# Expert rows gathered in quarters with dealt channels, and turned by VectorE instead of TensorE

## What is computed

```python
h = rmsnorm(x, g_norm_ffn) * (1.0 + sc2) + sh2          # one row of 1024 channels a token
lg = x @ w_router_grp + b;  gsel = argmax(lg)            # 1 of 4 groups
le = x @ w_router_exp + b   # the 8 experts of the group, softmax, top 2, weights renormalised
for e in range(32):                                      # SwiGLU, EXPERT_FF = 256
    hid = silu(x @ w_exp_gate[e]) * (x @ w_exp_up[e])
    out = out + combine[:, e:e + 1] * (hid @ w_exp_down[e])
x = x + gt2 * out;  y = rmsnorm(x, g_final)
```

## Time and profile before

| | |
|---|---|
| median of 3 runs | 1409.73 us (1407.08, 1409.73, 1416.6) |
| the profiled execution | 1413.11 us |
| its span in the trace | 1411.4 us |
| mean granted TensorE clock | 0.973 of 2.4 GHz |
| TensorE busy | 1327.9 us (94%), weight loads 795.0 us |
| VectorE, ScalarE, POOL busy | 606.3 us, 323.3 us, 117.9 us |
| moved | 243.47 MB in 121473 packets, mean 173 GB/s |
| out projection to slot table | 890 to 1052 us of the span |
| the 23 rounds | first product at 1060.95, last at 1333.58 |
| loop block and final norm | to the end |

### The profile page before, as it was taken

One profiled execution on the slowest core, in us unless ns is written; L12 is line 12 of the kernel. 1 busy time (PEld: TensorE's weight loads), 2 busy tenths in 40 slices (PEclk: granted clock), 3 DMA queues, 4 the chain that ended last, 5 costly groups with the idle time before them and its releaser, 6 DMA issues. The chain is left out here.

```text
span 1411.4 us, 21105 instructions
## 1 busy us (share of the span) xinstructions
PE 1327.9 (94%) x8689; PEld 795.0 (56%) x8689; DVE 606.3 (43%) x1290; ACT 323.3 (23%) x692; POOL 117.9 (8%) x135
## 2 busy tenths in 40 slices
PE   5899999999999999999999999999959999999976
PEld 3344448876667666666567666788853333333322
DVE  6743452324342144950482244434653632222247
ACT  4200002545443210122322222111211011111013
POOL 0000001030000051010000000000010000000042
PEclk9999999999999999999999999999968999999997
DMA  9425324321002362422413084610076999999878
GB/s 363 126 90 166 110 90 157 126 78 42 27 19 74 99 213 72 148 62 61 84 56 141 16 272 121 232 64 31 30 276 231 365 374 408 418 417 414 344 244 240
DMA packets 121473, 243.47 MB, mean 173 GB/s; under 512 B 23159, under 2 KB 87303, under 8 KB 112137
## 3 DMA queue, kind: packets, MB, share of 16 engines
q1 hardware_dynamic: 98368, 191.69, 38.1%
q10 hardware_dynamic: 14690, 28.26, 5.4%
q0 software_dynamic: 8320, 22.17, 5.2%
HBM read 208.30 MB, written 37.07 MB: 174 GB/s over the span
## 5 line engine op out<-in xcount | busy, mean ns | idle before, releaser
L2419 PE MATMUL psum<-ring,big 128*128 128x256 f32 x512 | 117.4, 388 | 0.0
L1308 PE MATMUL psum<-h_t,ring 128*128 128x352 f32 x368 | 111.4, 461 | 1.1 <-ACT gate_units L1599 1.1
L2419 PEld LDWEIGHTS psum<-ring,big 128*128 128x128 f32 x512 | 98.4, 195 | 14.1 <-issue 0.4
L2558 PE MATMUL psum<-w_gate_up,u_rows 128*32 128x512 f32 x608 | 101.7, 609 | 2.8 <-ACT u_rows L2707 1.1
L2558 PE MATMUL psum<-ring,u_rows 128*32 128x512 f32 x576 | 101.7, 599 | 1.3 <-ACT u_rows L2707 0.9
L1308 PEld LDWEIGHTS psum<-h_t,ring 128*128 128x128 f32 x368 | 69.0, 190 | 38.3 <-issue 1.6
L2580 PE MATMUL psum<-big 128*32 128x512 f32 x736 | 83.7, 595 | 0.0
L469 PE MATMUL psum<-big,u_rows 128*128 128x512 f32 x144 | 63.9, 593 | 0.0
L2100 PE MATMUL psum<-big,h_t 128*128 128x352 f32 x192 | 60.5, 459 | 1.9 <-PEq L2053 1.9
L2717 ACT ACTIVATE big<-psum 128x256 f32<-128x256 f32 x23 | 8.8, 385 | 232.3 <-PE psum L2558 232.3
L3069 DVE TENSOR_SCALAR v_new<-u_rows,v_new 128x512 f32<-128x512 f32 x46 | 25.1, 546 | 81.5 <-PE psum L2580 80.6
(11 more groups left out here) (540 smaller groups left out, 2125.5 us busy)
## 6 DMA issues: line engine op xcount, KB each, us to landing
big<-in_w_exp_down SPq DMA_DIRECT2D x32, 1024.0 KB, 16.3
ring<-in_w_ada SPq DMA_DIRECT2D x24, 1024.0 KB, 7.8
w_gate_up<-in_w_exp_gate SPq DMA_DIRECT2D x13, 1024.0 KB
w_gate_up<-in_w_exp_up SPq DMA_DIRECT2D x13, 1024.0 KB
ring<-in_w_exp_gate SPq DMA_DIRECT2D x13, 1024.0 KB
ring<-in_w_exp_up SPq DMA_DIRECT2D x13, 1024.0 KB
ring<-in_w_in SPq DMA_DIRECT2D x11, 1024.0 KB, 10.2
h_t<-tmp_gates SPq DMA_DIRECT2D x48, 176.0 KB, 2.6
```

The lines of the kernel that those rows point to most:

```text
L1308: m = T_.matmul(bank[4 + u % 4][:, 0:CW], w_[:, k, c0:c0 + P], ht3[:, k, j * CW:(j + 1) * CW], start=(k == 0), stop=(k == KT - 1))
L2419: m = T_.matmul(bank[2 * (i % 2) + b // 2][0:r, (b % 2) * WB:(b % 2 + 1) * WB], merged_t[:, k, t * P:t * P + r], w[:, k, :], start=(k == 0 ...
L2558: m = T_.matmul(bank[i][at, :], x_t[i][:, k * P + CHUNK * c:k * P + CHUNK * (c + 1)], w_gu[use_of(e, GSLOTS)[0]][:, :, k, :], start=(k == ...
```

## The change

The row of a token is written to `tmp_h_rows` in another channel order, and fetched and turned in another way:

- In `tile` and `last_tile` the normalised row is stored as [quarter q][j][d] with channel 256 q + 8 d + j ("dealt"): inside a quarter, 32 channels eight apart come side by side. The multiply becomes four instructions of 256 elements (two per half in `last_tile`) that read `x2` and the gain with a stride of 8; the addition reads the shift with that stride. ACT's stores are as before.
- The router weights `w_r` are loaded in the same order, by 16 DMAs on SP instead of 2, before the sample rows.
- VectorE computes `quarter_i` (4 * token + q, 16 small operations behind the slot table), four of them for each chunk x. `gather(b)` is four indirect DMAs of 128 pieces of 1 KB: partition 32 q + s of column block x takes quarter q of the row of slot 32 x + s.
- `turn_x` moves to VectorE: one transpose in 32x32 blocks of 128x1024, from `xg` straight to `x_t`. TensorE's turns in the loop, their two PSUM banks and ACT's `copy_x` are gone. VectorE's order is turn_x(b + 1), hidden(b), ...
- SP's load of expert 4 waits for the first round's gather alone. POOL waits for VectorE's turn where it waited for TensorE's.
- `turn_loop_x` brings the loop block's rows into natural partition order with 32 products against the identity (4 column groups of 32) instead of 8 transposes.

```diff
@@ load of the router weights (SP)
-                sp.dma_start(w_r[:, :, 0:NG], I["w_router_grp"][0].rearrange("(k p) e -> p k e", p=P)).then_inc(s_rt, 16)
-                sp.dma_start(w_r[:, :, NG:NG + NE], I["w_router_exp"][0].rearrange("(k p) e -> p k e", p=P)).then_inc(s_rt, 16)
+                for name, c0, c1 in (("w_router_grp", 0, NG), ("w_router_exp", NG, NG + NE)):
+                    for j in range(KT):
+                        at = slice(CHUNK * (j % 4), CHUNK * (j % 4 + 1))
+                        sp.dma_start(w_r[at, j // 4:KT:2, c0:c1], I[name][0].rearrange("(q d j) e -> j d q e", q=4, j=KT)[j]).then_inc(s_rt, 16)
...
-                sp.wait_ge(s_xg[0], 16)
-                sp.wait_ge(s_xg[1], 16)
+                sp.wait_ge(s_xg[0], 64)
@@ POOL
                 def gather(b):
-                    G.indirect_dma_start(xg[b % 2], None, scratch["h2_rows"],
-                                         bass.IndirectOffsetOnAxis(ap=tok_i[:, b:b + 1], axis=0),
-                                         bounds_check=N - 1, oob_is_err=False).then_inc(s_xg[b % 2], 16)
+                    for x in range(4):
+                        if b == 0:
+                            pool.wait_ge(s_ix, x + 1)
+                        G.indirect_dma_start(xg[b % 2][:, WB * x:WB * (x + 1)], None, scratch["h2_rows"].rearrange("n (q c) -> (n q) c", q=4),
+                                             bass.IndirectOffsetOnAxis(ap=quarter_i[:, x, b:b + 1], axis=0),
+                                             bounds_check=4 * N - 1, oob_is_err=False).then_inc(s_xg[b % 2], 16)
@@ TensorE
-                def turn_x(b):
...
-                    for k in range(KT):
-                        m = T_.transpose(bank[2 + k // 4][:, (k % 4) * P:(k % 4 + 1) * P], xg[i][:, k:D:KT], ident[:, :])
...
-                            m = T_.matmul(bank[i][at, :], x_t[i][:, k * P + CHUNK * c:k * P + CHUNK * (c + 1)],
+                            m = T_.matmul(bank[i][at, :], x_t[i][:, WB * c + CHUNK * k:WB * c + CHUNK * (k + 1)],
...
-                        m = T_.transpose(bank[2 + k // 4][:, (k % 4) * P:(k % 4 + 1) * P], lx[:, k:D:KT], ident[:, :])
+                        for q in range(4):
+                            m = T_.matmul(bank[2 + k // 4][CHUNK * q:CHUNK * (q + 1), (k % 4) * P:(k % 4 + 1) * P],
+                                          lx[:, WB * q + CHUNK * k:WB * q + CHUNK * (k + 1)], ident[:, :], start=True, stop=True)
@@ VectorE, tile(i); last_tile the same in halves of two pieces
+        def dealt(x):
+            return x.rearrange("p (q d j) -> p q j d", d=CHUNK, j=KT)
+        def as_stored(x):
+            return x.rearrange("p (q j d) -> p q j d", d=CHUNK, j=KT)
...
-                    c.step(dve, V.scalar_tensor_tensor(out=h2, in0=x2_of(t)[0:r, :], scalar=ss5[0:r, t:t + 1], in1=rows_["gain2"][0:r, :],
-                                                       op0=ALU.mult, op1=ALU.mult))
-                    V.tensor_tensor(h2, h2, rows_["shift2"][0:r, :], ALU.add).then_inc(s_h2, 1)
+                    for q in range(4):
+                        m = V.scalar_tensor_tensor(out=as_stored(h2)[:, q], in0=dealt(x2_of(t)[0:r, :])[:, q], scalar=ss5[0:r, t:t + 1],
+                                                   in1=dealt(rows_["gain2"][0:r, :])[:, q], op0=ALU.mult, op1=ALU.mult)
+                    c.step(dve, m)
+                    V.tensor_tensor(as_stored(h2), as_stored(h2), dealt(rows_["shift2"][0:r, :]), ALU.add).then_inc(s_h2, 1)
@@ VectorE, behind the slot table, and the turn
+                dve.wait_ge(s_map, 1)
+                for x in range(4):
+                    for q in range(4):
+                        m = V.tensor_scalar(quarter_i[CHUNK * q:CHUNK * (q + 1), x, :], tok_i[CHUNK * x:CHUNK * (x + 1), :], 4.0, float(q), ALU.mult, ALU.add)
+                    m.then_inc(s_ix, 1)
...
+                def turn_x(b):
+                    dve.wait_ge(s_xg[b % 2], 64 * (b // 2 + 1))
+                    if b >= 2:
+                        dve.wait_ge(s_gup, b - 1)
+                    V.transpose(x_t[b % 2], xg[b % 2]).then_inc(s_txc, 1)
...
+                turn_x(0)
                 for b in range(ROUNDS):
+                    if b + 1 < ROUNDS:
+                        turn_x(b + 1)
                     hidden(b)
```

More of the change, by code:

```diff
@@ L2129, in build @@
         tok_i = sb("token_of_slot", [P, ROUNDS], I32)
+        quarter_i = sb("row_quarter_of_slot", [P, 4, ROUNDS], I32)
         w_slot = sb("weight_of_slot", [P, ROUNDS])
@@ L2232, in build @@
         s_yst = [sem(f"expert_rows{i}_stored") for i in range(2)]
-        s_tx, s_txc, s_sil, s_hid = sem("x_t_in_psum"), sem("x_t_copied"), sem("gate_activated"), sem("hidden_ready")
+        s_ix, s_txc, s_sil, s_hid = sem("row_quarters_known"), sem("x_turned"), sem("gate_activated"), sem("hidden_ready")
         s_th, s_thc, s_dna, s_dnd = (sem("hidden_t_in_psum"), sem("hidden_t_copied"),
@@ L2362, in _ @@
                     if b >= 2:
-                        pool.wait_ge(s_tx, b - 1)
+                        pool.wait_ge(s_txc, b - 1)
                     gather(b)
-                pool.wait_ge(s_tx, ROUNDS - 1)
+                pool.wait_ge(s_txc, ROUNDS - 1)
                 pool.wait_ge(s_ovr, 1)
@@ L2447, in route @@
                     if i == 0:
-                        pe.wait_ge(s_rt, 32)
+                        pe.wait_ge(s_rt, 32 * KT)
                     if i >= 1:
@@ L2529, in _ @@
                 find_last()
-                def turn_x(b):
[L2532 to L2535, removed]
-                    for k in range(KT):
-                        m = T_.transpose(bank[2 + k // 4][:, (k % 4) * P:(k % 4 + 1) * P], xg[i][:, k:D:KT], ident[:, :])
-                    m.then_inc(s_tx, 1)
                 def experts_of(b):
@@ L2593, in members @@
                     T_.matmul(MEMBERS, ones, total[:, :], start=True, stop=True).then_inc(s_rank, 1)
-                turn_x(0)
                 for b in range(ROUNDS):
@@ L2599, in _ @@
                         members()
-                    if b + 1 < ROUNDS:
-                        turn_x(b + 1)
                     if b >= 1:
@@ L2612, in turn_loop_x @@
                     for k in range(KT):
-                        m = T_.transpose(bank[2 + k // 4][:, (k % 4) * P:(k % 4 + 1) * P], lx[:, k:D:KT], ident[:, :])
+                        for q in range(4):
+                            m = T_.matmul(bank[2 + k // 4][CHUNK * q:CHUNK * (q + 1), (k % 4) * P:(k % 4 + 1) * P],
+                                          lx[:, WB * q + CHUNK * k:WB * q + CHUNK * (k + 1)], ident[:, :], start=True, stop=True)
                     m.then_inc(s_ltx, 1)
-                pe.wait_ge(s_txc, ROUNDS)
                 turn_loop_x(0)
@@ L2701, in _ @@
                 exponentials(2)
[L2703 to L2707, removed]
                 def copy_loop_x(n):
@@ L2722, in store @@
                     act.dma_start(scratch["expert_rows"][P * b:P * (b + 1), :], y_e[b % 2]).then_inc(s_yst[b % 2], 16)
-                copy_x(0)
                 for b in range(ROUNDS):
@@ L2728, in _ @@
                     silu(b)
-                    if b + 1 < ROUNDS:
-                        copy_x(b + 1)
                     if b == ROUNDS - 1:
@@ L2835, in last_tile @@
                     for at in halves:
-                        c.step(dve, V.scalar_tensor_tensor(out=h2[:, at], in0=x2[:, t, at], scalar=ss5[:, t:t + 1], in1=row_p["gain2"][:, at],
-                                                           op0=ALU.mult, op1=ALU.mult))
-                        V.tensor_tensor(h2[:, at], h2[:, at], row_p["shift2"][:, at], ALU.add).then_inc(s_h2, 1)
+                        for q in range(2):
+                            m = V.scalar_tensor_tensor(out=as_stored(h2[:, at])[:, q], in0=dealt(x2[:, t, at])[:, q], scalar=ss5[:, t:t + 1],
+                                                       in1=dealt(row_p["gain2"][:, at])[:, q], op0=ALU.mult, op1=ALU.mult)
+                        c.step(dve, m)
+                        V.tensor_tensor(as_stored(h2[:, at]), as_stored(h2[:, at]), dealt(row_p["shift2"][:, at]), ALU.add).then_inc(s_h2, 1)
                 def take_logits(i):
```

1 line of the change is left out of this document (removed).

## The result

The changed kernel took **1418.6 us** (median of 17 runs, sixteen of them 1411.0 to 1424.2) against 1411.2 for the kernel before (17 runs): ratio 1.0056, 95% interval 1.0043 to 1.0070. In a second set it was 1.0063 (1.0041 to 1.0084). So: slower by 0.6%, forecast 1418. In each of the two sets of 17 one run took far longer (3417.8 and 1984.5 us), and range, ratio and interval are without them.

What follows compares the result with a forecast made beforehand. TensorE was taken to bound the out projection and early rounds, DMA the rounds from about 1160 us on. 8.9 - 3.3 + 3.4 - 1.1 + 0.9 = +8.8 us on the median 1409.7 gave 1418.5; predicted 1418, range 1405 to 1431.

Steps and rivals of the forecast that it cites:

- Tile stage: Tiles before the slot table: dealt writing adds 2.1 us a tile (multiply pieces 0.66, addition 1.96); +8.9 us shows.
- First gather and turn: Slot table to first product: small VectorE operations, four gather issues instead of one, and VectorE's turn; +3.0 us.
- Quarter rows: The 20 or so rounds with full DMA: 1 KB pieces move slower than 4 KB, +0.17 us each; +3.4 us.
- Last landing: Last weight load's arrival: release after round 2's down product moves by -1.1, DMA idle time gives 2.2; -3.3 us.
- Turn behind the last landing: Round 21: TensorE's turn removed behind the last weight load's arrival, a plain 1.1 us gained.
- the loop turn: Loop block's turn before the last down product: 32 products take 1.75 us instead of 0.89; +0.9 us.
- A: Rounds: loads keep up, so rounds follow TensorE and all its turns are won; 1399 us, chance 0.06.
- B: Tile stage: dealt order costs nothing extra, strided reads at full rate; 1411 us, 1408 with the gather free; chance 0.20.
- C: Rounds 3 to 21: quarter rows crowd the DMA engines, 18 us instead of 3.4; 1433 us, chance 0.17.

Runs made afterwards that it cites:

- experiment 2: Changed kernel with natural channel order in tiles, router weights and loop turn; VectorE's transpose reads gathered quarter rows with the stride: 1407.8 us, 0.9998 of the kernel before.
- experiment 6: Kernel before, with SyncE's load of expert 4 waiting for the first gather alone, not the first two: 1407.8 us, ratio 0.9984.
- experiment 8: Kernel before, with quarter gathers and VectorE's strided turns in rounds 1 to 8 alone, natural order, expert 4's load waiting for the first gather alone: 1404.5 us, ratio 0.9962.
- the light before of 5: Kernel before, without loads of half the gate and up weights of experts from 5 on: 1407.4 us, 0.9980 of the kernel before.
- the filled kernel 2 of 7: Experiment 2's kernel with 16 dead TensorE transposes ahead of the weight wait in rounds 6, 9, 12, 15, 18 and 21: 1408.8 us, 0.9985 of the kernel before.
- experiment 1: Kernel before, with only the dealt writing of the tiles' rows and the router weights loaded in that order: 1419.0 us, ratio 1.0057.
- experiment 3: Changed kernel with one gather of whole 4 KB rows a round in place of four of 1 KB: 1413.6 us, 1.0028 of the kernel before.
- experiment 4: Changed kernel with eight dead TensorE transposes of the identity put into each round: 1422.6 us, 1.0079 of the kernel before.
- the light after: Changed kernel without loads of half the gate and up weights of experts from 5 on: 1389.2 us, 0.9873 of the kernel before.
- the filled one: Changed kernel with 16 dead TensorE transposes ahead of the weight wait in rounds 9, 12, 15, 18 and 21: 1419.3 us, 1.0065 of the kernel before.
- experiment 5: Kernel before and changed kernel, both without loads of half the gate and up weights of experts from 5 on: 1407.4 and 1389.2 us.

## Why the prediction was right, point by point

**Tile stage, +8.9: right, with a spread that I had not seen.** The prices were 0.66 and 1.96, measured 0.677 and 2.015 (experiment 2 gives the old ones back). For the stage as a whole I took the start of the out projection to the start of the slot table in every trace. Six with the natural order (before, experiments 2, 6 and 8, the light before of 5 and the filled kernel 2 of 7) all give 164.9 us. Seven with the dealt order (after twice, 1, 3, 4, the light after and the filled one) give 170.2, 170.3, 170.3, 173.6, 176.3, 176.3 and 176.3: mean 173.3, **+8.4**. The steps between them are the clock. The chain (start us, us, what) of the kernel before and of the second trace of the changed one:

```profile
887.19 13.83 PE psum L2419 x64
...
991.47 8.59 PE psum L2419 x32
...
1011.80 8.66 PE psum L2419 x32
```

```profile
883.89 13.83 PE psum L2430 x64
...
997.74 8.59 PE psum L2430 x32
...
1018.06 8.66 PE psum L2430 x32
```

32 matmuls that take 6.9 us at the full clock take 8.6 in two places of each; the first trace of the changed kernel has neither. So its 170.2 stands against 164.9 less 2 x 1.7 = 161.5: +8.7 at an equal clock. The trace with 173.6 is also 8.7 above 164.9; from 985 to 1010 its mean granted clock is 0.93, as before. The three of 176.3 have 0.86 there.

The tiles bear the working out one by one. In the first trace of the changed kernel, up to where the clocks part:

```profile
932.46 1.09 PE psum L2452 x8
...
993.53 1.97 PE psum L2463 x16
```

These are the turns of tile 2 and the sixth router product, 47.5 and 108.6 us behind the start of the out projection, where the kernel before has 43.6 and 101.7: +3.9 and +6.9. The forecast's terms up to there add up to 4.3 and 7.0. In between, tiles 3 and 4 are 4.3 and 4.7 late (4.6 and 4.9 forecast).

**First gather and turn, +3.0: too much, +1.3.** The issue was delayed by 0.75 (1.91 after the slot table instead of 1.16; I had 0.5), and the fourth issue left 4.07 behind the first (I had 4.3). The failed step is the landing: I let the last quarter take the 4.59 us of the whole gather, and it took 2.78. The turn took 1.25 (I had 1.2).

**Quarter rows, +3.4 of DMA: not settled.** The rates say 3 to 4 us, experiment 3 leaves 1.6, the pace of the late rounds shows none above its scatter. The Trainium skill (DMA: Bandwidth & Descriptors, Specifications) would have made the term zero by its line rate from 512 B a transfer up; the rates speak against that, without proving it.

**Last landing, −3.3: the step is right, the size too small; −4.8 to −5.6.** The forecast had put it together from −4.1 for four turns, −2.2 for DMA's idle time behind them and +3.0 for the first gather. The load behind round 2's down product, which the forecast had taken as the release, left 57.0 us behind the slot table before (1052.08 to 1109.10), and 52.1 and 53.7 after: −3.4, if the first is freed of the 1.5 us by which its round 0 ran at a better clock (8.4 us instead of 9.9). Of that, +1.3 is the first gather, so the four turns gave 4.7; in experiment 8, which has them alone, the same load is 4.8 earlier. The idle time did get filled: share 0.97 from 1110 to 1160 in the kernel before, 1.01 after and 1.02 in experiment 8. That makes −3.4 − 2.2 = −5.6. By the times, experiment 8 gained 6.1 us in the median (interval 2.7 to 8.2); with +1.3 for the first gather that leaves −4.8.

**Turn behind the last landing, −1.1, and the loop turn, +0.9:** by the chain, the rounds 21 and 22 are 10.88 apart (12.10 before: −1.2); the loop turn takes 1.89 (+1.0).

**The sum.** With −4.8 and with 3.5 for the quarter rows it is 8.4 − 4.8 + 3.5 − 1.2 + 1.0 = +6.9; with −5.6 and 1.6 it is +4.2. The medians say +7.4 in both sets, the ratios +7.9 and +8.9, the forecast +8.8. The terms behind the slot table, which the forecast had at −0.1 together, thus add up to −1.5 or −4.2. Two readings of them as a whole differ. The times say about zero, within some 3 us: +8.0 for the dealt order alone, +7.9 and +8.9 for everything. The traces say −4 to −5: from the slot table to the end it is 353.9 and 355.2 us in the changed kernel and 359.3 in the one before. But these are three single executions; experiment 1, in which nothing changed behind the table, took 357.8 there, so 1.5 us of it is scatter, and the rest stays open. So the total came out for the right reason in its one large term, the tile stage. That it came within 1.5 us is in part luck: of the terms behind the table, the first gather was 1.7 too dear, four turns were 0.6 to 0.7 too cheap and the quarter rows perhaps too dear, all in the same direction.

**Rivals.** A needs transfers that keep up; experiment 5 makes them keep up, and the changed kernel wins; experiment 4 shows that here they do not. B fell with the pieces' durations, 677 and 2015 ns. The Trainium skill (SBUF — State Buffer, Door 1) lets floats stride only 4 apart freely; these durations at 8 apart agree, and no run tried 4. C's mechanism, if it is there, has at most a fifth of its price. The prediction also held that a change under 1% can't be told from none; with 17 runs of each kernel 0.6% could.

## What to carry to other kernels

Where two engines take turns as the limit, a gain on one is worth only what the other still had idle before it became full; the same 24 us of TensorE work, put back, cost some 3 us here, and taking them away was worth some 25 with a third of the transfers gone. Use the new form only where the relieved engine sets the pace: with 8 of the 23 rounds in it experiment 8 measured 0.9962, with all of them experiment 2 measured 0.9998 (the intervals just overlap). A layout that a later step needs belongs where an engine has room: the same stride cost 2.2 us a tile in front of TensorE and next to nothing beside it. And before reading half a per cent from two traces, line up a stretch that the change leaves alone and look at its clock: four of seven traces of the dealt tile stage were 3 to 6 us longer by that alone.

## What the runs showed of the hardware

- A VectorE transpose of 128x1024 floats in 32x32 blocks took 1.24 us, as long as a plain addition of that size (1225 ns); reading with a stride of 8 floats, 2.06.
- The stride's price was much the same in the three operations: +0.77 to +0.81 ns an element, once, though two operands of the multiply are read so. (Addition 2015 − 1225 over 1024; transpose 2063 − 1238 over 1024; multiply 677 − 480 over 256.)
- An indirect gather held POOL's queue 1.0 us whatever its rows were (998 ns for 1 KB rows, 989 for 4 KB); in the first round the last of four quarter gathers, the others already under way, landed in 2.8 us, where the whole one had taken 4.6.
- With TensorE waiting up to 6 us for weights every third round, its granted clock fell from 2.4 to 1.2 GHz in or right behind three of the waits, in both traces of the changed kernel (0.50 from 1205 to 1211), and the 64 matmuls behind took 8.8 to 9.3 us instead of 7.07. One wait of 3.3 us passed without a fall (product at 1168.75, 7.07 us). With waits of about 2 us at most it went either way: it stayed full from 1110 to 1310 before and in experiment 8 (longest wait 2.1 us), and fell once in experiment 6 (8.77 us at 1317.73, behind a wait of 1.8) and once in experiment 4 (8.77 at 1255.87, behind 2.1).
